# A mixture of experts in quarter blocks: four experts share one block, and the norm tiles of two projections are re-staged

## The chip, the cores and the metric

The kernel runs on one core of one Trainium2 chip. A core has TensorE (PE, matmuls into PSUM), VectorE (DVE), ScalarE (ACT), GpSimd (POOL) and SyncE (SP, which only issues DMAs here), and 16 DMA engines. The metric is the device time of one execution in microseconds; the median of three runs is shown. All data are fp32. An "fp32r" matmul is a faster one on rounded operands: three of them on high and low parts stand for one full fp32 product. A plain fp32 matmul with 512 moving columns appears in the trace as two records.

## The reference

Two blocks follow each other on 1024 tokens of 1024 channels. The part that changes most is the mixture of experts of the first block:

```python
scores = sigmoid(h @ router_w)                  # 64 experts
_, top_e = top_k(masked(scores + router_b), 8)  # 8 experts for each token
gate = gate / sum(gate) * 2.5
# tokens sorted by expert, in blocks of one expert each
def step(out, (tok, gw, e)):
    y = (silu(h[tok] @ wg[e]) * (h[tok] @ wu[e])) @ wd[e] * gw[:, None]
    return out.at[tok].add(y), None
return swiglu(h, shared) + routed
```

wg and wu are 1024 x 256 for each expert, wd 256 x 1024: 3.15 MB an expert, 201 MB for all. Before it come the first block's projection (rmsnorm, then `@ w_in`), two recurrences (rwkv and hgrn) and the output projection; behind it `x + g2 * moe`, a norm, and the second block, which begins with another rmsnorm and `@ w_in_2`.

## The kernel before

The program is a row of stages, each with its own instruction order written out by hand for every engine, tied by semaphores. Between stages all engines meet. The stages that matter here:

- `project_first` (names `front_`). It has two halves of 640 tokens. For each half, five tiles of 128 rows (one of them smaller) are normed by ScalarE and VectorE (`norm`), turned by TensorE into PSUM (`turn`, L530), and split into `a_high` and `a_low`. Then `product(s)` goes over the column tiles of the weight, two column halves c of 24 fp32r matmuls each (L548), into the banks `ps`; further banks, `aux`, serve the small lora products in between. The turned rows are put into `ps` too, so a half's turning waits until all products of the half before are taken out.
- `output_route` (names `out_`). It is the output projection, the second norm, the router, and the table that lists for each expert the tokens that chose it. An expert has room for 1024 tokens, rows of 128 places. SP loads the rows of tile i+3 while tile i is computed.
- `shared_expert`. It has the shared expert's matmuls in plain fp32 (L2324). It stores its result into `total` in DRAM; meanwhile VectorE turns the counts into the table of blocks: `owner[j]`, the expert of block j, `slots[:, j]`, its 128 tokens, and `done[e]`, the first block of expert e. Places that no token fills point at a row behind the last.
- `routed_experts` (names `routed_`, and `moe_exp_w` for the ring with the weights of four experts). It always runs 127 blocks, the number that the worst routing could need. Each block has 128 slots of one expert. Blocks behind the last used one belong to expert 63 and do unused work. In block j, TensorE turns the 128 gathered rows of block j+1 (L2526, 8 transposes), multiplies block j's x by the up and gate weights (L2559: 8 depth tiles by three fp32r products, x stationary with 128 columns, 512 weight columns moving, into `p_gu`), then block j−1's hidden rows by the down weights (L2541 and L2542), and turns block j's hidden rows (L2568). ScalarE rounds the weights to `w_high` (L2585, four pieces) and `wd_high`, VectorE subtracts to `w_low` (L2649) and `wd_low`. GpSimd gathers rows three blocks ahead (L2494, indirect DMA) and adds each result into `total` by an indirect DMA that accumulates (L2503). SP refills a ring entry when `done` says that its expert's last block has been used, the up and gate weights first, then the down weights.
- the second block's projection (names `pre_`). For each of eight tiles VectorE multiplies `total` with a gain and adds `x` (L3655, L3667), norms it twice, and TensorE turns it (L3523); then come the products (L3510). Products of two weight tiles are placed between the last turns. GpSimd splits these weights.

## Time and profile before

| | |
|---|---|
| median of 3 runs | 4236.89 us (4229.92 to 4244.08) |
| profiled execution, its own time | 4234.69 us |
| its span | 4232.8 us, mean granted clock 0.935 |
| PE / DVE / ACT / POOL busy | 86% / 63% / 48% / 21% |
| moved by DMA | 690.96 MB, 163 GB/s |
| loop over the experts | from 1794 to 3094 us |

The span is from the first to the last instruction. Busy time is a union per engine; a matmul's end is modelled, and overlapping ones make the "mean ns" of one longer than the distance of two starts. The slices of the page are 105.8 us each. PEclk is the granted TensorE clock, 1.00 being 2.4 GHz and 0.50 1.2 GHz.

### The profile page before, as it was taken

How to read it: one execution, taken by the hardware profiler on the slowest of the kernel's cores; microseconds unless marked ns; L12 is line 12 of the kernel's file. 1: busy time of each engine (PE TensorE's matmuls, PEld its weight loads, DVE VectorE, ACT ScalarE, POOL GpSimd, SP SyncE). 2: the span in 40 equal slices, each digit the busy share in tenths (PEclk: the TensorE clock that was granted, in tenths of full speed). 3: DMA queues.
4: the chain of work that ended last, by engine and by line, in shares of the span. 5: the costliest groups of instructions: out<-in, count | busy, mean ns of one | idle time of the engine just before them, and what ended most of it. 6: DMA issues, size and time to landing. Idle time of an engine off the chain costs nothing. (4 is left out here: it accounts for less than half of the span.)

```text
span 4232.8 us, 93615 instructions
## 1 busy us (share of the span) xinstructions
PE 3643.4 (86%) x35448; PEld 2938.0 (69%) x35449; DVE 2676.3 (63%) x4120; ACT 2044.4 (48%) x2837; POOL 907.3 (21%) x799
## 2 busy tenths in 40 slices
PE   4899799678776679799999999999949989968779
PEld 0898788577676557377777677777737767856667
DVE  2588688555555566287777777777768666036731
ACT  1477576322222153077777777777742222136720
POOL 3000000134433003323223233322213333300000
PEclk6899899799899789899999999999969999989989
DMA  8254344322210635499999999754563421355552
GB/s 302 76 172 155 116 159 153 128 68 56 81 54 9 216 136 138 154 318 270 277 342 341 341 338 340 190 108 108 111 168 90 119 75 60 110 139 134 131 169 80
DMA packets 527112, 690.96 MB, mean 163 GB/s; under 512 B 77904, under 2 KB 424656, under 8 KB 523728
## 3 DMA queue, kind: packets, MB, share of 16 engines
q1 hardware_dynamic: 487232, 545.70, 40.5%
q0 software_dynamic: 39088, 139.12, 13.4%
q8 instruction: 240, 3.93, 0.4%
q10 hardware_dynamic: 480, 1.62, 0.1%
q14 instruction: 72, 0.59, 0.0%
HBM read 508.35 MB, written 178.00 MB: 162 GB/s over the span
## 5 line engine op out<-in xcount | busy, mean ns | idle before, releaser
L2649 DVE TENSOR_TENSOR routed_w_low<-moe_exp_w,routed_w_high 128x1024 fp32r<-128x1024 f32 x512 | 603.0, 1219 | 26.8 <-ACT routed_w_high L2585 23.5
L2585 ACT CAST routed_w_high<-moe_exp_w 128x1024 fp32r x512 | 510.9, 1045 | 61.7 <-DMA moe_exp_w<-in_exp_w_up_dram 26.0
L2503 POOL DMA_INDIRECT total<-routed_y,routed_yidx x127 | 238.0, 1874 | 825.6 <-ACT routed_y L2610 304.4
L2559 PE MATMUL routed_p_gu<-routed_w_high,routed_x_high 128*128 128x512 f32 x1016 | 415.0, 408 | 0.0
L2559 PE MATMUL routed_p_gu<-routed_w_low,routed_x_high 128*128 128x512 f32 x1016 | 404.1, 398 | 0.0
L2559 PE MATMUL routed_p_gu<-routed_w_high,routed_x_low 128*128 128x512 f32 x1016 | 404.0, 398 | 0.0
L548 PE MATMUL front_ps<-front_a_high,front_w_high 128*128 128x320 f32 (+1 forms) x1120 | 363.5, 325 | 16.7 <-DVE front_w_low L785 13.5
L548 PE MATMUL front_ps<-front_a_high,front_w_low 128*128 128x320 f32 (+1 forms) x1120 | 355.2, 317 | 0.0
L548 PE MATMUL front_ps<-front_a_low,front_w_high 128*128 128x320 f32 (+1 forms) x1120 | 355.0, 317 | 0.0
L3510 PE MATMUL pre_ps<-pre_a_high,pre_w_high 128*128 128x512 f32 x720 | 287.7, 400 | 15.3 <-ACT pre_xb L3644 6.6
L3510 PE MATMUL pre_ps<-pre_a_low,pre_w_high 128*128 128x512 f32 x720 | 281.7, 391 | 0.0
L3510 PE MATMUL pre_ps<-pre_a_high,pre_w_low 128*128 128x512 f32 x720 | 281.7, 391 | 0.0
L2542 PE MATMUL routed_p_y<-routed_wd,routed_hT_rest 128*128 x508 | 260.2, 593 | 0.0
L1427 POOL TENSOR_TENSOR rwmix_TT<-rwmix_at,rw_mask 64x256 f32<-64x256 f32 (+1 forms) x60 | 43.4, 724 | 944.4 <-DVE rwmix_at L1328 938.5
L548 PEld LDWEIGHTS front_ps<-front_a_high,front_w_high 128*128 128x128 f32 x1120 | 214.3, 191 | 35.5 <-DVE front_w_low L785 18.1
L2559 PEld LDWEIGHTS routed_p_gu<-routed_w_high,routed_x_low 128*128 128x128 f32 x1016 | 192.1, 189 | 46.7
L2559 PEld LDWEIGHTS routed_p_gu<-routed_w_low,routed_x_high 128*128 128x128 f32 x1016 | 192.9, 190 | 41.0
L2559 PEld LDWEIGHTS routed_p_gu<-routed_w_high,routed_x_high 128*128 128x128 f32 x1016 | 192.9, 190 | 41.1
L548 PEld LDWEIGHTS front_ps<-front_a_low,front_w_high 128*128 128x128 f32 x1120 | 214.2, 191 | 1.3
L548 PEld LDWEIGHTS front_ps<-front_a_high,front_w_low 128*128 128x128 f32 x1120 | 213.9, 191 | 0.0
L2494 POOL DMA_INDIRECT moe_xg<-yn,moe_idx x128 | 157.8, 1233 | 104.5 <-DVE moe_idx L2638 53.7
L3510 PEld LDWEIGHTS pre_ps<-pre_a_high,pre_w_high 128*128 128x128 f32 x720 | 136.2, 189 | 48.7 <-issue 18.1
(556 smaller groups left out, 8362.3 us busy)
## 6 DMA issues: line engine op xcount, KB each, us to landing
moe_exp_w<-in_exp_w_gate_dram SPq DMA_DIRECT2D x64, 1024.0 KB, 14.4
moe_exp_w<-in_exp_w_up_dram SPq DMA_DIRECT2D x64, 1024.0 KB, 19.3
routed_wd<-in_exp_w_down_dram SPq DMA_DIRECT2D x64, 1024.0 KB, 15.5
front_wt<-in_w_in_dram SPq DMA_DIRECT2D x70, 512.0 KB, 4.3
mod_w<-in_w_mod_dram SPq DMA_DIRECT2D x24, 1024.0 KB, 18.1
pre_wt<-in_w_in_dram SPq DMA_DIRECT2D x44, 512.0 KB, 4.1
out_a<-mix SPq DMA_DIRECT2D x24, 512.0 KB, 4.4
proj<-pre_xv SPq DMA_DIRECT2D x16, 512.0 KB, 2.6
```

Source lines behind the costliest of these rows:

```text
L548: op = nc.tensor.matmul(ps[:, s % 2, c, 0:size], w_part[:, s % 2, k, :], a_part[:, k, first + c * size:first + (c + 1) * size], start=(k = ...
L1427: nc.gpsimd.tensor_tensor(combos(TT[u][:])[to, es], combos(at[u][:])[at_rows, es], mask(MASK_LEVEL, at_rows, es), ALU.mult)
L2494: nc.gpsimd.indirect_dma_start(xg[:, b % 2, :], None, yn, bass.IndirectOffsetOnAxis(ap=idx[b][:, :], axis=0))\
L2503: nc.gpsimd.indirect_dma_start(total, bass.IndirectOffsetOnAxis(ap=yidx[b % 2][:, :], axis=0), y[:, b % 2, :], None, compute_op=ALU.add).t ...
L2542: op = nc.tensor.matmul(p_y[:, h, :], hT_rest[:, :], wd[:, bass.ds(e % WS, 1), 1, cols], start=False, stop=True)
L2559: op = nc.tensor.matmul(p_gu[:, :], x_part, w_part[:, k, :], start=(k == 0 and i == 0), stop=(k == KD - 1 and i == 2))
L2585: nc.scalar.copy(w_high[:, q * KQ:(q + 1) * KQ, :].rearrange("p k m -> p (k m)"), wgu[:, bass.ds(e % WS, 1), q * KQ:(q + 1) * KQ].rearrang ...
L2649: nc.vector.tensor_tensor(w_low[:, at, :].rearrange("p k m -> p (k m)"), wgu[:, bass.ds(e % WS, 1), at].rearrange("p o k j m -> p (o k j m)"),
L3510: op = nc.tensor.matmul(ps[:, u, a:a + n], w_part[:, u, k, :], a_part[:, k, a:a + n], start=(k == 0 and j == 0), stop=(k == KD - 1 and j = ...
```

## The change

**The loop over the experts.** Blocks of 128 slots become "quads": four quarters of 32 slots, each of its own expert (consecutive quarters in the sorted list, so often the same expert). Their number is 80, again the worst case. A matmul's stationary operand is now x of one quarter, 32 columns, and its result goes to 32 partitions of the PSUM bank: four matmuls in a row, for the spots 0 to 3, have the same depth and different columns of the array. All are plain fp32; the splits into high and low parts are gone. Only spot 0 reads its weights from the ring at an address in a register; those of the other three spots are copied to a fixed ring `fixed` of four steps, spot 1 by ScalarE, spots 2 and 3 by VectorE. A quad has six steps: four pairs of depth tiles on the way up, two on the way down; `chunk_done` counts them and frees the places. SP refills an entry after the quad that holds the expert's last quarter; up weights of expert e+3, then down weights of expert e.

**The sums.** The same token could stand in two quarters of one quad, so each spot adds into its own part of `total`. Parts 1 to 3 are cleared in `output_route` by three DMAs from a tile of zeros (1024 x 1024 fp32 each). The second block's norm loads all four parts of a tile and adds them on TensorE with the identity as stationary operand (`sums_of`), and VectorE takes the sum from PSUM.

**The table.** Its rows have 32 places; four indirect DMAs in place of one fetch them, and owners are turned four times.

**The first projection.** The turned rows go into the `aux` banks instead of `ps`. So `ps` is free under the norm, and the first column half of the first two weight tiles is computed before the last two turned tiles of each half. VectorE's `bonus` of the last column tile of the first half is moved ahead of the second norm, since it reads `aux`.

TensorE in the routed loop, one block of the kernel before, from the turns on (a block is an expert's 128 slots; w_high, w_low and x_high, x_low are the parts; the three products then come seven times more):

```order
L2568 MATMUL routed_p_h<-ident,routed_hid 128x128 x2
L2526 MATMUL routed_p_x<-ident,moe_xg 128x128 x8
L2559 MATMUL routed_p_gu<-routed_w_high,routed_x_high 128x512
L2559 MATMUL routed_p_gu<-routed_w_low,routed_x_high 128x512
L2559 MATMUL routed_p_gu<-routed_w_high,routed_x_low 128x512
```

and one quad of the kernel after, where moe_exp_w is spot 0's weight in the ring and routed_fixed those of spots 1 to 3 (this pair then comes seven times more):

```order
L2638 MATMUL routed_p_h<-ident,routed_hid 128x128 x2
L2589 MATMUL routed_p_x<-ident,moe_xg 128x128 x8
L2492 TENSOR_LOAD moe_owner
L2492 ISA x2
L2608 ISA
L2608 MATMUL routed_p_gu<-moe_exp_w,routed_x 32x512
L2608 MATMUL routed_p_gu<-routed_fixed,routed_x 32x512 x3
```

Three products of 128 columns give way to four of 32 for each depth tile.

VectorE in the same loop, from the turned rows' gates on; before (routed_w_low is the low part of a quarter of the up weights, routed_wd_low that of the down weights):

```order
L2642 COPY routed_gate<-moe_xg 128x1
L2643 TENSOR_TENSOR routed_x_low<-routed_p_x,routed_x_high 128x1024
L2638 CAST moe_idx<-moe_slots 128x1
L2458 TENSOR_LOAD moe_owner
L2458 ISA x2
L2656 ISA
L2656 TENSOR_TENSOR routed_wd_low<-routed_wd,routed_wd_high 128x1024
L2649 ISA
L2649 TENSOR_TENSOR routed_w_low<-moe_exp_w,routed_w_high 128x1024
```

and after, around the multiplication that makes the hidden rows:

```order
L2742 ISA
L2742 COPY routed_fixed<-routed_wd 128x1024
L2726 ISA x4
L2730 ISA
L2730 COPY routed_fixed<-moe_exp_w 128x1024
...
L2771 TENSOR_TENSOR routed_hid<-routed_sg,routed_p_gu 128x256
L2748 CAST routed_yidx<-moe_slots 128x1
```

Each step has two copies where it had one subtraction, and an address in a register before each; behind the last row six more such copies follow.

TensorE in the second block's norm; before, five turned tiles stand together ahead of the first product:

```order
L3523 MATMUL pre_aux<-ident,pre_yb 128x128 x40
L3510 MATMUL pre_ps<-pre_a_high,pre_w_high 128x512
```

and after, with the sums of the four parts (pre_buf and pre_wide hold the parts of even and odd tiles):

```order
L3619 MATMUL pre_ps<-pre_buf,ident 128x512 x8
L3619 MATMUL pre_ps<-pre_wide,ident 128x512 x8
L3635 MATMUL pre_aux<-ident,pre_yb 128x128 x8
L3619 MATMUL pre_ps<-pre_buf,ident 128x512 x8
L3635 MATMUL pre_aux<-ident,pre_yb 128x128 x8
L3619 MATMUL pre_ps<-pre_wide,ident 128x512 x8
```

The sum of tile t+1 stands behind the turn of tile t−1 and ahead of the turn of tile t.

The diff, cut to its core:

```diff
@@ project_first, tensor
             def turn(half):
                 if half:
-                    pe.wait_ge(evicted, PER)
+                    pe.wait_ge(aux_act, 5 * QT)
+                    pe.wait_ge(aux_dve, 2 * QT)
                 for j, (src, idx) in enumerate(sources[half]):
                     t, size = half * NT + j, src.shape[0]
+                    if j >= NT - 2:
+                        early(half * PER + j - (NT - 2))
                     pe.wait_ge(y_made, t + 1)
...
+            def early(s):
+                pe.wait_ge(w_split, s + 1)
+                if s >= PER:
+                    pe.wait_ge(evicted, s - 1)
+                pe.wait_ge(low_made, s // PER * NT + 3)
+                columns(s, 0)
@@ output_route, sync
+                if 1 <= i < SPOTS:
+                    sp.dma_start(total[i * PART:i * PART + SEQ, :].rearrange("(p r) (a l) -> p (r a) l", p=P, l=P),
+                                 none[:].rearrange("p (o l) -> p o l", o=1).broadcast_to([P, SEQ * D // P // P, P])).then_inc(none_sent, 16)
@@ sizes
-BLOCKS = SEQ * TOP_K // P + N_EXPERTS
-USED = (SEQ * TOP_K + (P - 1) * N_EXPERTS + N_EXPERTS - TOP_K) // P
+SPOTS = 4
+QUARTER = P // SPOTS
+QUADS = (SEQ * TOP_K + (QUARTER - 1) * N_EXPERTS + N_EXPERTS - TOP_K) // QUARTER // SPOTS + 1
+PART = SEQ + QUARTER
@@ routed_experts, sync
+            def next_first(e, at, w):
+                quad = sp.value_load(tb["done"][0:1, at], min_val=0, max_val=NB - 2)
+                sp.wait_ge(chunk_done, quad * STEP + CH)
+                first(e, w)
+            def next_second(e, at, w):
+                quad = sp.value_load(tb["done"][0:1, at], min_val=0, max_val=NB - 2)
+                sp.wait_ge(chunk_done, quad * STEP + 2 * STEP)
+                second(e, w)
...
+                    next_first(i * WS + (w + WS - 1), only(i * WS + w), (w + WS - 1) % WS)
+                    next_second(i * WS + w, only(i * WS + (w - WS + 1)), w)
@@ routed_experts, tensor
+            def up(j, b):
+                e = owner(pe, j, 0)
+                pe.wait_ge(x_made, j + 1)
...
+                for c in range(CH):
+                    copies(up_step(j, c))
+                    for k in range(c * KC, (c + 1) * KC):
+                        cols = slice((k - c * KC) * BANK, (k - c * KC + 1) * BANK)
+                        for s in range(SPOTS):
+                            w = wgu[:, bass.ds(e % WS, 1), k * BANK:(k + 1) * BANK] if s == 0 else fixed[:, place_of(b, c), s - 1, cols]
+                            op = nc.tensor.matmul(p_gu[spot(s), :], x[:, b % 2, k, spot(s)], w, start=(k == 0), stop=(k == KD - 1))
...
+                for m in range(MT):
+                    copies(down_step(j, m))
...
+                            op = nc.tensor.matmul(p_y[spot(s), h, :], hT[:, m, spot(s)], w, start=(m == 0), stop=(m == MT - 1))
@@ routed_experts, vector
+            def up_copies(es, j, b, c):
+                g = up_step(j, c)
...
+                    dve.wait_ge(chunk_done, g - (R - 1))
+                for s in (2, 3):
+                    op = nc.vector.tensor_copy(fixed[:, place_of(b, c), s - 1, :],
+                                               wgu[:, bass.ds(es[s] % WS, 1), c * D:(c + 1) * D].rearrange("p o n -> p (o n)"))
@@ second block's projection, tensor
+            def sums_of(t):
+                pe.wait_ge(parts_ready[t % 2], 16 * SPOTS * (t // 2 + 1))
+                if t >= 1:
+                    pe.wait_ge(part_made, t)
+                for a in range(2):
+                    for j in range(SPOTS):
+                        op = nc.tensor.matmul(ps[:, a, BANK:2 * BANK], consts["ident"][:, :], parts_t[t % 2][j][:, a * BANK:(a + 1) * BANK],
+                                              start=(j == 0), stop=(j == SPOTS - 1))
+                op.then_inc(summed, 1)
@@ second block's projection, vector
             def gained(t):
-                dve.wait_ge(x_ready[t % 4], 32 * (t // 4 + 1))
-                nc.vector.tensor_tensor(total_t[t % 4][:, :], total_t[t % 4][:, :], gain_row[:, :], ALU.mult).then_inc(part_made, 1)
+                dve.wait_ge(summed, t + 1)
+                for a in range(2):
+                    cols = slice(a * BANK, (a + 1) * BANK)
+                    op = nc.vector.tensor_tensor(spread[:, t % 2, cols], ps[:, a, BANK:2 * BANK], gain_row[:, cols], ALU.mult)
```

## Rows read from the trace of the kernel before

**Rows 1.** The page: TensorE's busy tenths and GB/s in 40 slices.
```profile
PE   4899799678776679799999999999949989968779
GB/s 302 76 172 155 116 159 153 128 68 56 81 54 9 216 136 138 154 318 270 277 342 341 341 338 340 190 108 108 111 168 90 119 75 60 110 139 134 131 169 80
```

**Rows 2.** Windows of the loop: busy us (count) by engine, granted clock, DMA share, GB/s.
```profile
core 0: us, PE busy (x) PEld busy (x) DVE busy (x) ACT busy (x) POOL busy (x), PEclk, DMA share, GB/s
2094.00:2194.00 100.00, 93.81 (x413) 70.23 (x412) 71.48 (x102) 69.06 (x93) 27.59 (x18) 0.98 1.07 338
...
2860.00:3060.00 200.00, 200.00 (x897) 151.91 (x896) 156.13 (x224) 154.47 (x205) 56.88 (x41) 1.00 0.50 108
```

**Rows 3.** Timeline of TensorE over one block: start, length, instruction.
```profile
2809.70 1.04 PE L2526 MATMUL routed_p_x<-ident,moe_xg 128*128 128x128 f32 x8
2810.49 0.48 PE L2559 MATMUL routed_p_gu<-routed_w_high,routed_x_high 128*128 128x512 f32 x1
...
2816.20 0.39 PE L2541 MATMUL routed_p_y<-routed_wd_high,routed_hT_high 128*128 128x512 f32 x1
...
2819.30 0.38 PE L2568 MATMUL routed_p_h<-ident,routed_hid 128*128 128x128 f32 x2
2819.52 0.71 PE L2526 MATMUL routed_p_x<-ident,moe_xg 128*128 128x128 f32 x5
```

**Rows 4.** The page's costliest groups: count, busy us, mean ns, idle before.
```profile
L2649 DVE TENSOR_TENSOR routed_w_low<-moe_exp_w,routed_w_high 128x1024 fp32r<-128x1024 f32 x512 | 603.0, 1219 | 26.8 <-ACT routed_w_high L2585 23.5
L2585 ACT CAST routed_w_high<-moe_exp_w 128x1024 fp32r x512 | 510.9, 1045 | 61.7 <-DMA moe_exp_w<-in_exp_w_up_dram 26.0
L2503 POOL DMA_INDIRECT total<-routed_y,routed_yidx x127 | 238.0, 1874 | 825.6 <-ACT routed_y L2610 304.4
...
L2494 POOL DMA_INDIRECT moe_xg<-yn,moe_idx x128 | 157.8, 1233 | 104.5 <-DVE moe_idx L2638 53.7
```

**Rows 5.** Timeline of TensorE at four places: rows of equal matmuls.
```profile
999.91 0.67 PE L1144 MATMUL rwmix_ps<-rwmix_TT,rwmix_W 64*64 64x64 f32 x30
...
1767.78 19.05 PE L2324 MATMUL shared_pd<-shared_wd,shared_hid 128*128 128x512 f32 x44
...
3804.94 1.31 PE L2893 MATMUL attn_po<-attn_pT,attn_v 128*64 128x128 f32 x20
...
3951.83 1.39 PE L3172 MATMUL ssd_pb<-ssd_sq,ones 128*128 128x128 f32 x11
```

**Rows 6.** Groups of TensorE by form, for the mean length of one.
```profile
L1144 PE MATMUL rwmix_ps<-rwmix_TT,rwmix_W 64*64 64x64 f32 x3200 | 73.0, 225 | 14.8 <-DVE rwmix_W L1344 9.7 <-issue 5.0
...
L2893 PE MATMUL attn_po<-attn_pT,attn_v 128*64 128x128 f32 x576 | 38.5, 278 | 0.8 <-DVE attn_res L2944 0.5
...
L2324 PE MATMUL shared_pd<-shared_wd,shared_hid 128*128 128x512 f32 x64 | 27.7, 592 | 0.0
...
L3172 PE MATMUL ssd_pb<-ssd_sq,ones 128*128 128x128 f32 x128 | 17.3, 293 | 2.4 <-ACT ssd_sq L3228 2.4
```

**Rows 7.** One tile of the second projection: ns min/median/max, first and last start.
```profile
L3724 DVE TENSOR_SCALAR pre_buf<-pre_aux x8: 1217/1224/1225, 3228.8 to 3332.2; 128x1024 f32<-128x1024 f32 x8
...
L3734 DVE TENSOR_SCALAR pre_buf<-pre_buf x4: 693/694/695, 3376.4 to 3574.4; 128x1024 f32<-128x1024 f32 x4
```

**Rows 8.** Timeline of VectorE and GpSimd in the second norm.
```profile
3127.33 3.13 POOL L3502 TENSOR_TENSOR pre_w_low<-pre_wt,pre_w_high 128x1024 fp32r<-128x1024 f32 x1 [0.15 <-issue]
...
3128.30 3.25 DVE L3671 TENSOR_TENSOR pre_xv<-pre_xb,pre_xc 128x1024 f32<-128x1024 f32 x1
```

**Rows 9.** DMA issues of the loop: count, KB each, median us to landing.
```profile
routed_wd<-in_exp_w_down_dram SPq DMA_DIRECT2D x64, 1024.0 KB, 15.5
```

**Rows 10.** Timeline of TensorE in the second norm, with its wait.
```profile
3144.19 1.97 PE L3523 MATMUL pre_aux<-ident,pre_yb 128*128 128x128 f32 x8 [4.68 <-DVE pre_yb L3685]
3150.84 1.97 PE L3523 MATMUL pre_aux<-ident,pre_yb 128*128 128x128 f32 x8 [4.69 <-DVE pre_yb L3685]
```

**Rows 11.** Windows of 10 us in the three norms (columns as in rows 2).
```profile
120.00:130.00 10.00, 8.44 (x43) 8.28 (x43) 1.31 (x3) 1.87 (x2) 0.00 (x0) 0.64 0.28 77
...
450.00:460.00 10.00, 5.13 (x24) 4.58 (x25) 6.93 (x10) 4.76 (x7) 0.00 (x0) 0.50 0.21 72
...
3140.00:3150.00 10.00, 1.97 (x8) 1.57 (x8) 9.40 (x14) 7.30 (x12) 0.00 (x0) 0.50 0.74 202
```

More of the change, by code:

```diff
@@ L2248, in shared_expert @@
         cnt_i = st.sb("cnt_i", [P, 2, NE], I32)
-        nb, cmp, end, start, one = (st.sb(n, [P, NE]) for n in ("nb", "cmp", "end", "start", "one"))
-        lane = st.sb("lane", [P, 1])
-        own = st.sb("own", [P, 5])
-        row = st.sb("row", [P, 1], U32)
+        nb, end, start, one = (st.sb(n, [P, NE]) for n in ("nb", "end", "start", "one"))
+        cmp = st.sb("cmp", [P, SPOTS, NE])
+        lane, behind = st.sb("lane", [P, SPOTS]), st.sb("behind", [P, 1])
+        own = st.sb("own", [P, 5, SPOTS])
+        row = st.sb("row", [P, SPOTS], U32)
         places = st.sb("places", [P, P])
@@ L2317, in _ @@
             pe.wait_ge(own_made, 1)
-            nc.tensor.transpose(own_row, own[:, 0:1], consts["ident"][:, :]).then_inc(turned, 1)
+            for j in range(SPOTS):
+                op = nc.tensor.transpose(own_row[:, j * P:(j + 1) * P], own[:, 0, j:j + 1], consts["ident"][:, :])
+            op.then_inc(turned, 1)
             for c in range(DOWN):
@@ L2347, in _ @@
             nc.vector.memset(one[:, :], 1.0)
-            nc.vector.memset(tb["slots"][:, BLOCKS:, :], 0.0)
-            nc.vector.memset(tb["owner"][0:1, BLOCKS:], NE - 1)
+            for j in range(SPOTS):
+                nc.vector.memset(behind[j * QUARTER:(j + 1) * QUARTER, :], float(j * PART))
             for c in range(BEGUN):
@@ new lines, in down @@
+            def down(j, b):
+                e = owner(pe, j, 0)
+                pe.wait_ge(hT_made, j + 1)
+                if not begins(j):
+                    pe.wait_ge(y_made, j)
+                for m in range(MT):
+                    copies(down_step(j, m))
+                    at = place_of(0, m) if ends(j) else place_of(b + 1, CH + m)
+                    for h in range(2):
+                        cols = slice(h * BANK, (h + 1) * BANK)
+                        for s in range(SPOTS):
+                            w = wd[:, bass.ds(e % WS, 1), m, cols] if s == 0 else fixed[:, at, s - 1, cols]
+                            op = nc.tensor.matmul(p_y[spot(s), h, :], hT[:, m, spot(s)], w, start=(m == 0), stop=(m == MT - 1))
+                    op.then_inc(chunk_done, 1)
@@ L2562, in body @@
-                if not first:
-                    down(j - 1)
+                if not ends(j):
+                    turn(j + 1, (b + 1) % BS, r + (b + 1) // BS)
+                up(j, b)
+                if not begins(j):
+                    down(j - 1, (b - 1) % BS)
                 pe.wait_ge(hid_made, j + 1)
-                if not first:
-                    pe.wait_ge(h_split, j)
+                if not begins(j):
+                    pe.wait_ge(hT_made, j)
                 for k in range(MT):
@@ new lines, in down_copies @@
+            def down_copies(j, b):
+                e, last = owner(act, j, 1), owner(act, j, SPOTS - 1)
+                for w in range(WS):
+                    act.wait_ge(second_loaded[w], (last + (WS - w)) // WS * 16 + (16 if w else 0))
+                for m in range(MT):
+                    act.wait_ge(chunk_done, down_step(j, m) - (R - 1))
+                    at = place_of(0, m) if ends(j) else place_of(b + 1, CH + m)
+                    nc.scalar.copy(fixed[:, at, 0, :], wd[:, bass.ds(e % WS, 1), m, :].rearrange("p o n -> p (o n)"))\
+                        .then_inc(first_copied, 1)
@@ L2664, in _ @@
             indices(2, 2)
[L2665 to L2668 removed]
+            es = [owner(dve, 0, s) for s in range(SPOTS)]
+            gates(es, 0, 0)
+            for c in range(CH):
+                up_copies(es, 0, 0, c)
             def body(j, b, r):
[L2671 removed]
+                es = [owner(dve, j + 1, s) for s in range(SPOTS)]
                 if not isinstance(j, int) or j >= BS - 1:
```

396 lines of the change are left out of this document (210 added, 186 removed).

## The prediction

> **What bounds the kernel now.** I read the busy slices of the page first [rows 1]: the longest stage with a constant picture is slices 17 to 29, where TensorE is at 9 of 10 throughout. That is the loop over the chosen experts. The windows cut it up [rows 2]: it runs from 1794 to 3094 us, 1300 us, 31% of the span. Its second half (2860 to 3060) has TensorE busy for all of 200 us at 108 GB/s. From 2094 it has 338 GB/s and more and TensorE is short of full by 6%. So TensorE bounds the loop, and while weights still arrive the DMA nearly does.
>
> The timeline of one block [rows 3] gives the price of a block: from one set of turns (2809.70) to the next (2819.52) 9.82 us. The multiplications start 0.234 us apart, from 2810.49 to 2816.20 for 24 of them. The loop runs 127 blocks [rows 4]: 127 × 9.82 = 1247, and 53 us are start and stalls. VectorE and ScalarE are at 78 and 77% there.
>
> The profiled execution's own time is 4234.7 us (span 4232.8), 2 us under the median of 4236.9. I count against 4234.7.
>
> **The loop: TensorE per quad.** A quad is 128 slots of up to four experts. The turns of x and of the hidden rows stay: 2810.49 − 2809.70 = 0.79, and 0.22 for the two others [rows 3]. In place of 24 fp32r multiplications and 8 for the way down come 32 and 16 in plain fp32, each 32 columns wide with 512 moving. What would one cost alone? 44 recorded halves of such multiplications take 19.05 us, the last of them 0.59 [rows 5, 6]: (19.05 − 0.59)/43 = 0.429 us a half, 0.858 for the whole. The question on which everything hangs is how many of the four run side by side. Recorded halves on a whole array with 128 moving columns stand (1.39 − 0.29)/10 = 0.110 us apart; those of attention, on two column halves at full depth, (1.31 − 0.27)/19 = 0.055: two abreast, nothing lost. The rwkv ones, on 64 × 64 tiles, stand (0.67 − 0.22)/29 = 0.0155 apart with 64 moving columns, where one alone would need 0.055: 3.5 abreast [rows 5, 6]. No row shows four column tiles at full depth. Bounds: 12 steps × 0.858 = 10.3 us if four run together, 20.6 if two do. I take 10.3, since nothing is lost with two at full depth and four have run at once, and 11.8 (10.3 × 4/3.5) as the poor end. A quad is then 10.3 + 0.79 + 0.22, with 0.1 for changes of tile form, 11.4 us; 80 quads (the new count) are 912 us instead of 1247.
>
> The Trainium skill (TensorE: Matmul & The Clock Gate, "Part 3: Packing small matmuls") measures 2.38 times for three column tiles, and 10.6 for sixteen. By 2.38/3 a quad would be 10.3/0.79 + 1.1 = 14.1 us and the total, worked out as below, 4192; this trace has two tiles without such a loss, and does not show four.
>
> **The loop: copies.** The splits into high and low parts go; three of the four experts' weights are copied into a fixed ring, 6 chunks of 128x1024 a quad. ScalarE copies one expert: 6 × 1.045 [rows 4]. Its block of now is 9.82 × 0.77 = 7.6 us [rows 2] with five such casts, so one more makes 8.7. VectorE copies two: 12 copies. The nearest rows, one input in SBUF and 128x1024, take 0.694; the same from PSUM 1.22 [rows 7]. I take 0.69, since the copies are from SBUF: 8.3, and seven small operations, 1.3 in all: 9.6 us. Both lie under TensorE's 11.4. VectorE's bad end is 12 × 1.22 + 1.3 = 15.9. Before a copy's address is known the engine loads the owner into a register, six loads instead of two on VectorE; I leave 1 us for them, still under 11.4.
>
> **The loop: DMA.** A block gathers and scatters 1.08 MB (108 GB/s in the windows × 9.82), a quad the same. An expert's weights are 3.15 MB. At the ceiling of 340 GB/s [rows 2] and 13 us a quad, 83 GB/s go to rows and 257 to weights: 12.2 us an expert. The first half of the loop now runs at that ceiling. The reference's own routing gives these inputs 26 to 455 tokens an expert: 288 quarters, so 72 of the 80 quads hold tokens. 24 experts have 5 or more quarters (40.25 quads, TensorE sets 11.4 × 40.25 = 459), 40 have four or fewer (the DMA sets 40 × 12.2 = 488), 8 empty quads 91: 1038. The ring looks three experts ahead, which evens some of it out; against that, a down weight is now queued behind the next 2 MB, and lands in 15.5 us already now [rows 9], where it has one quad. I add 20 for it and 12 for the start: 1070. The term: 1070 − 1300 = −230 us. Its bounds: −375 if only TensorE counts (912 + 12), −110 if each small expert costs another 3 us.
>
> **The second block's norm.** The four partial sums are added on TensorE, 16 halves of 0.429 a tile: 6.9 us at 2.4 GHz, 13.7 at 1.2. The cycle of a tile is 3150.84 − 3144.19 = 6.65 us now [rows 10], with TensorE waiting. In the order after, the sum of tile t+1 stands behind the turn of t−1, VectorE takes it before it finishes tile t, and the next turn waits for that: 0.8 + 6.9 + 1.4 (two of 128x512 from PSUM, half of 1.22 each and a little) + 1.5 + 0.4 = 11.0. Seven cycles × 4.35 = 30. The two products that fill waits now (24 × 0.234 = 5.6 each) are no longer hidden: 11. The first two sums run where the granted clock is 0.50 [rows 11]: 19. Sum +60; +45 if they are partly hidden, +100 if the clock stays at 1.2 GHz.
>
> **Zeros.** Three further parts are cleared, 12.6 MB, 37 us at 340 GB/s, from the same queue as the rows of the output projection. That stage moves 138 GB/s [rows 1] and loads three tiles ahead. +5, from 0 to +37. What is fetched in four pieces behind the table costs +3.
>
> **The first projection.** Under each of the two norms the first columns of two weight tiles move into TensorE's waits. Now it stands idle or turns rows at a granted 0.50 until about 121 and 460 us [rows 11]. Moved are 2 × 24 multiplications at 320/512 of 0.234, 7 us at each norm, 14 in all; the last turned rows are now queued behind them, and VectorE's norm behind those, which I put at 1 us each: −12, from −20 to +2 (if the norm chain is delayed by as much as was moved).
>
> Sum: 4234.7 − 230 + 60 + 5 + 3 − 12 = 4060.7; the median of runs stood 2 us above: **4062 us**.
>
> **Rivals.**
> - *Two abreast.* The four matmuls of a step share the array only in pairs: 21.7 us a quad, 80 × 21.7 + 12 = 1748, total 4235 + 448 + 56 = 4739. For it: no row has more than two column tiles on one set of rows. Against it: four rwkv tiles at once. It makes the kernel slower from 15.4 us a quad on (1244 for the loop). 9%.
> - *VectorE and GpSimd on each other.* While GpSimd ran a 3.13 us operation, a VectorE one of 1.22 took 3.25 [rows 8]. GpSimd's two indirect DMAs take 1.23 + 1.87 us a quad [rows 4]. If VectorE's copies drop to 1.22, it is 80 × 15.9 + 12 = 1284, total 4275, slower; it decides from 1.17 a copy. If the two only take turns, VectorE's 10.6 and GpSimd's 3.1, it is 13.7 a quad, 1108 for the loop, 4101 in all. Against both: the subtractions take 1.219 on average with GpSimd's DMAs beside them [rows 4]. Copies at 1.22: 6%; turns: 4%.
>  The Trainium skill (SBUF — State Buffer, "SBUF: two separate sides") says that an fp32 copy on VectorE locks GpSimd out of a shared port, and measures an indirect-style DMA at 3100 instead of 620 ns. Five times 3.1 would be 15.5 us a quad and 4243 in all. The trace has no such copy beside an indirect DMA.
> - *A short pack.* Four tiles reach 3.5, as the rwkv ones did: 12.9 us a quad, 40.25 × 12.9 + 488 + 8 × 12.9 + 32 = 1142, total 4135. For it: those same rows. Against it: their matmuls are an eighth as long, so a fixed cost weighs more. 10%.
> - *The DMA is no bound.* The ring evens out large and small experts: 924, total 3915. For it: averaged, 190 + 78 MB at 340 GB/s are 788 us, less than TensorE's 821 for 72 quads. 8%.
> - *DMA queues bind more than I count*: 1190, total 4181. For it: weights now land after 15.5 us. 11%.
> - My forecast: 52%.
>
> **Chances and range.** Of the 85 that lie on the fast side (forecast 52, queues 11, short pack 10, no DMA bound 8, turns 4) I leave 3 for several bad bounds meeting, so that nothing measurable is left: faster 82%, no change 3% (0.3%, 13 us, is what a measurement tells here). Slower 15%: two abreast 9, VectorE at 1.22 6. The range takes the forecast with the bounds of its terms and all cases but the slower ones: 3910 to 4210.
>
> **What would show it.** The multiplications of the loop in groups of four within about 20 ns, the groups 0.43 us apart; or pairs. Quads 11.4 us apart from the 72nd on, and 12 to 14 before, with DMA at 340 GB/s and TensorE waiting for copies whose releaser is a weight's DMA. VectorE's copy at 0.69. In the norm, tiles 11 us apart with sums in between. The first columns before the last turned rows. It would be wrong if quads without tokens stood more than 12.8 apart, or if VectorE were never idle in the loop.

## The result and the profile after

| | before | after |
|---|---|---|
| median of 6 runs each | 4233.41 us (4228.34 to 4257.26) | 4261.5 us (4256.74 to 4263.24) |
| ratio to before, 95% interval | | 1.0055 (1.0034 to 1.0076) |
| span / own time of the profiled execution | 4232.8 / 4234.7 | 4254.7 / 4257.0 |

The changed kernel is slower by 0.55%. I had forecast 4062 us. From where each stage starts and ends on the two timelines, the stages take:

| stage, us | before | after | difference | forecast |
|---|---|---|---|---|
| first projection and rwkv, to the end of rwkv | 1379.5 | 1357.4 | −22 | −12 |
| output projection and routing, to the shared expert | 177.7 | 206.7 | +29 | +5 |
| shared expert | 62.1 | 63.4 | +1 | +3 |
| loop over the chosen experts | 1301 | 1248 | −53 | −230 |
| second projection | 614.3 | 674.8 | +60.5 | +60 |
| all else (attention, ssd) | | | +6 | 0 |

The page of the kernel after: TensorE is no longer at 9 throughout in the loop (slices 17 to 28), the granted clock is below full there, and in slices 21 to 25 the DMA, at 338 to 342 GB/s before [rows 1], now moves 243 to 319.

```profile
PE   4998999587775877788868877889779999968779
...
PEclk6999999899897888899988988899889999989889
...
GB/s 302 93 156 173 113 178 128 129 68 54 77 41 76 158 210 169 158 266 195 169 319 249 243 283 275 223 215 116 130 181 86 119 76 64 105 140 141 120 168 79
...
q14 instruction: 162, 1.33, 0.1%
```

The question on which I said everything hangs was answered as forecast. Timeline of TensorE in the loop after: start, length, instruction (the second row stands for three). A group of four starts within 20 ns, the next 0.43 us later.

```profile
2799.50 0.59 PE L2608 MATMUL routed_p_gu<-moe_exp_w,routed_x 128*32 x1
2799.51 0.61 PE L2608 MATMUL routed_p_gu<-routed_fixed,routed_x 128*32 128x512 f32 x3
2799.93 0.59 PE L2608 MATMUL routed_p_gu<-moe_exp_w,routed_x 128*32 x1
```

The groups that answer to [rows 4]: the copies are as short as I took them (685 and 689 ns), GpSimd's scatter is shorter than before, and what is new is how long TensorE and VectorE stand ahead of what concerns `routed_wd`, the down weights.

```profile
L2623 PE MATMUL routed_p_y<-routed_wd,routed_hT 128*32 x640 | 353.5, 705 | 233.8 <-DVE routed_fixed L2742 226.0
...
L2730 DVE COPY routed_fixed<-moe_exp_w 128x1024 f32 x640 | 403.5, 685 | 32.0 <-PE routed_p_y L2623 25.4
...
L2742 DVE COPY routed_fixed<-routed_wd 128x1024 f32 x320 | 200.2, 689 | 299.1 <-DMA routed_wd<-in_exp_w_down_dram 182.0
...
L2565 POOL DMA_INDIRECT total<-routed_y,routed_yidx x80 | 126.5, 1581 | 901.4 <-ACT routed_y L2679 867.1
```

The waits from 1900 to 3000 by what ended them (us in total, times, longest) show that ScalarE stands there too:

```profile
ACT routed_fixed L2673 <- DMA routed_wd<-in_exp_w_down_dram: 234.2, 24, 19.1
PE routed_p_y L2623 <- DVE routed_fixed L2742: 206.2, 30, 15.9
DVE routed_fixed L2742 <- DMA routed_wd<-in_exp_w_down_dram: 163.6, 24, 18.1
```

One of those waits on the timeline of all engines. SyncE asks for gate and up weights of an expert three ahead at 1866 and only then, at 1870.45, for down weights; they are there at 1887. TensorE, done with its up step at 1873, waits 16 us and then takes 0.85 us a group instead of 0.43.

```profile
1866.63 2.57 SPq L2514 DMA_DIRECT2D moe_exp_w<-in_exp_w_up_dram  x1
...
1870.45 7.45 SPq L2518 DMA_DIRECT2D routed_wd<-in_exp_w_down_dram  x1
...
1887.60 2.50 DVE L2742 COPY routed_fixed<-routed_wd 128x1024 f32 x4 [18.38 <-DMA routed_wd<-in_exp_w_down_dram]
...
1889.29 1.06 PE L2623 MATMUL routed_p_y<-routed_wd,routed_hT 128*32 x1 [15.97 <-DVE routed_fixed L2742]
...
1890.14 1.06 PE L2623 MATMUL routed_p_y<-routed_wd,routed_hT 128*32 x1
```

The windows there (us, busy by engine, granted clock, DMA share, GB/s) show the clock at 1.00 before the wait and at 0.50 behind it, that is 1.2 instead of 2.4 GHz; this wait cost more than its length.

```profile
1866.00:1873.00 7.00, 7.00 (x67) 2.06 (x65) 2.29 (x8) 2.47 (x4) 2.55 (x2) 1.00 1.07 371
1889.00:1892.00 3.00, 2.71 (x16) 0.76 (x20) 3.00 (x7) 2.53 (x4) 0.00 (x0) 0.50 1.08 371
```

### The profile page after: what moved, and what is told of

Read it like the earlier page. It is cut to its first block and busy times, and to the rows that moved or that the text cites. A ratio compares the mean times of both kernels' runs of the same rounds, so it can differ in the third digit from the quotient of the medians.

```text
span 4254.7 us, 100492 instructions
## 1 busy us (share of the span) xinstructions
PE 3463.0 (81%) x38463; PEld 2353.4 (55%) x38464; DVE 2362.8 (56%) x4246; ACT 1763.5 (41%) x2362; POOL 716.3 (17%) x706
## 3 DMA queue, kind: packets, MB, share of 16 engines
q14 instruction: 162, 1.33, 0.1%
## 5 line engine op out<-in xcount | busy, mean ns | idle before, releaser
L2608 PE MATMUL routed_p_gu<-routed_fixed,routed_x 128*32 128x512 f32 x3840 | 567.3, 595 | 0.0
L2608 PE MATMUL routed_p_gu<-moe_exp_w,routed_x 128*32 x1280 | 566.2, 595 | 0.7 <-DVE routed_fixed L2730 0.7
L2623 PE MATMUL routed_p_y<-routed_wd,routed_hT 128*32 x640 | 353.5, 705 | 233.8 <-DVE routed_fixed L2742 226.0
L2662 ACT COPY routed_fixed<-moe_exp_w 128x1024 f32 x320 | 334.0, 1046 | 261.2 <-PE routed_p_y L2623 162.0
L2730 DVE COPY routed_fixed<-moe_exp_w 128x1024 f32 x640 | 403.5, 685 | 32.0 <-PE routed_p_y L2623 25.4
L2742 DVE COPY routed_fixed<-routed_wd 128x1024 f32 x320 | 200.2, 689 | 299.1 <-DMA routed_wd<-in_exp_w_down_dram 182.0
L2623 PE MATMUL routed_p_y<-routed_fixed,routed_hT 128*32 128x512 f32 x1920 | 354.4, 704 | 0.0
L2608 PEld LDWEIGHTS routed_p_gu<-moe_exp_w,routed_x 128*32 128x32 f32 x1280 | 134.5, 110 | 351.0 <-issue 351.0
L2673 ACT COPY routed_fixed<-routed_wd 128x1024 f32 x160 | 164.8, 1045 | 287.5 <-DMA routed_wd<-in_exp_w_down_dram 253.2
L2565 POOL DMA_INDIRECT total<-routed_y,routed_yidx x80 | 126.5, 1581 | 901.4 <-ACT routed_y L2679 867.1
```

The costliest lines, as they stand in the source:

```text
L2565: nc.gpsimd.indirect_dma_start(total, bass.IndirectOffsetOnAxis(ap=yidx[b % 2][:, :], axis=0), y[:, b % 2, :], None, compute_op=ALU.add).t ...
L2608: op = nc.tensor.matmul(p_gu[spot(s), :], x[:, b % 2, k, spot(s)], w, start=(k == 0), stop=(k == KD - 1))
L2623: op = nc.tensor.matmul(p_y[spot(s), h, :], hT[:, m, spot(s)], w, start=(m == 0), stop=(m == MT - 1))
L2662: nc.scalar.copy(fixed[:, place_of(b, c), 0, :], wgu[:, bass.ds(e % WS, 1), c * D:(c + 1) * D].rearrange("p o n -> p (o n)"))\
L2673: nc.scalar.copy(fixed[:, at, 0, :], wd[:, bass.ds(e % WS, 1), m, :].rearrange("p o n -> p (o n)"))\
L2730: op = nc.vector.tensor_copy(fixed[:, place_of(b, c), s - 1, :], wgu[:, bass.ds(es[s] % WS, 1), c * D:(c + 1) * D].rearrange("p o n -> p ( ...
```

## The experiments

Ratios are to the kernel before on the same chip, with their 95% interval. The times of stages come from each kernel's one profile.

### The loop: what a quad costs, and the down weights

**e2_no_weights.** Edit: `first(e, w)` and `second(e, w)` in the loop become `sp.sem_inc(loaded[w], 32)` and `sp.sem_inc(second_loaded[w], 16)`.

> Leaves out the loading of the routed experts' weights but for the first four experts (the first four's are used for all); copies, multiplications, gathers and scatters stay. It measures what the quads cost without weight traffic. By my sum 80 quads at 11.4 us and 12 us of start: 924 us. If four column tiles side by side or the copies cost more than I worked out, it is 1000 us or more; if copies or the scatters set the pace, the quads stand 12 us or more apart.

Measured: 4058.95 us in one run, loop 1053 us. Neither account fits alone: the distance from one quad's turns to the next is 11.68 us, near my 11.4, but every fourth is 17.1 to 18.7. The timeline of VectorE over three of the quads: ahead of its first work in a new round of the loop it stands 4.80 us, where the others have 1.33 and 0.95; ahead of the copies for the way down (L2742) it stands 1.9 to 2.6 us each time.

```profile
2413.06 0.62 DVE L2719 COPY routed_gate<-moe_xg 32x1 f32 x4 [1.33 <-issue]
...
2415.76 2.50 DVE L2742 COPY routed_fixed<-routed_wd 128x1024 f32 x4 [1.89 <-issue]
...
2424.42 0.62 DVE L2719 COPY routed_gate<-moe_xg 32x1 f32 x4 [0.95 <-ACT routed_y L2679]
...
2427.22 2.50 DVE L2742 COPY routed_fixed<-routed_wd 128x1024 f32 x4 [2.00 <-issue]
...
2439.72 0.62 DVE L2719 COPY routed_gate<-moe_xg 32x1 f32 x4 [4.80 <-issue]
...
2443.13 2.50 DVE L2742 COPY routed_fixed<-routed_wd 128x1024 f32 x4 [2.60 <-issue]
```

The DMA view of 2431 to 2440 has three pieces of instructions (packets, MB, share), which start at 2431.6, 2434.1 and 2436.6, just ahead of the restart at 2439.72; from 2400 to 2600 there are 19, five for each round of the loop, and in the same stretch of the kernel before the queue has no row at all.

```profile
q14 instruction: 3, 0.02, 1.0%
```

TensorE then waits for the copies, and its granted clock is 0.50 from 2443.4 to 2450.3:

```profile
2444.73 1.05 PE L2623 MATMUL routed_p_y<-routed_wd,routed_hT 128*32 x1 [3.77 <-DVE routed_fixed L2742]
...
2445.57 1.06 PE L2623 MATMUL routed_p_y<-routed_wd,routed_hT 128*32 x1
```

**e1_down_first.**

```diff
-                    next_first(i * WS + (w + WS - 1), ...)
                     next_second(i * WS + w, ...)
+                    next_first(i * WS + (w + WS - 1), ...)
```

> The changed kernel, with the down weights of an expert asked for ahead of the gate and up weights of the expert three further on (SyncE's two requests in the loop change places; same bytes, same instructions elsewhere). Theory, the order in the queue: the changed kernel asks for expert e's down weights only after e-1's last up chunk and behind 2 MB, where they are needed one quad later, though their slot had been free for long; TensorE then waits some 230 us for them. With the request earlier these waits go, and the loop falls from 1248 us to about 1050 (960 to 1080, my old sum without the 20 us for the queue), the total to about 4060. Rival, the bandwidth: the bytes can't come faster than they do, so the waits move to the gate and up weights, the loop stays above 1200 and the total above 4210.

Measured: 4137.69 us, ratio 0.9767 (0.9750 to 0.9784); loop 1135 us, 113 less than in the changed kernel. Shown: the order of two requests cost 113 us, and the bandwidth rival falls. VectorE's waits for down weights from 1900 to 2800, in the changed kernel and here:

```profile
DVE routed_fixed L2742 <- DMA routed_wd<-in_exp_w_down_dram: 153.5, 22, 18.1
...
DVE routed_fixed L2742 <- DMA routed_wd<-in_exp_w_down_dram: 60.9, 18, 10.3
```

I had expected 198 us and a loop of 1080 at most: a miss. The fourth quads that e2 showed are still there, at 17.2 to 25 us.

**e7_short_body** (on e1) **and e10_short_body_alone** (on the changed kernel). VectorE's loop body of four quads becomes one of two; index and gate columns are then addressed by a register:

```diff
-            turns(dve, body)
+            with dve.Fori(BS // PAIR, NB // PAIR - BS // PAIR) as i:
+                for b in range(PAIR):
+                    body(i * PAIR + b, b, i)
...
-                nc.vector.tensor_copy(idx[b][:, :], ...)
+                nc.vector.tensor_copy(idx_all[:, bass.ds(j % BS, 1)], ...)
```

> Down weights asked for first, and VectorE's loop over the quads written with a body of two quads instead of four (158 instructions of its list instead of 304; 36 returns to the loop's start instead of 18; the same operations in the same order, index and gate columns addressed by a register). Theory, the instructions: in the run without weight traffic each quad stands 11.68 us from the next but every fourth, where VectorE's loop starts over, stands 17.1 to 18.7; 8 KB pieces of instructions come in there, VectorE stands for 4.8 us, TensorE waits for its copies and goes on at half clock. The kernel before (134 instructions) has no such place. With a body that needs no fetching every quad is 11.68 apart, the loop falls from 1135 to about 1000 (960 to 1035: 80 x 11.68 + 12 = 946, and what the weights cost), the total to 4000 (3970 to 4040). Rival, the return itself: each return of a loop with registers to set costs VectorE some 4 us; twice as many returns then make the loop about 100 us longer, 1235. Second rival, VectorE is too full and loses its lead slowly: no change.

> The changed kernel with VectorE's shorter body alone, down weights still asked for last. If the two causes add, the loop falls from 1248 us by what the body costs, 17 or 18 times 6 to 9 us: about 1120 (1090 to 1150), total about 4135. If the waits for the down weights hide the fetching (VectorE waits there anyway), it falls by less than 60 us.

Measured: e7 4066.15 us, ratio 0.9606 (0.9582 to 0.9629), loop 1056; e10 4187.62 us, ratio 0.9894 (0.9869 to 0.9918), loop 1174. Both loops are longer than the ranges I gave. The two causes add: the short body is worth 79 us with the down weights asked for first and 74 without, the order 118 with the short body and 113 without. The pieces of instructions are gone from the loop (76 over the whole span instead of 162), and the rival of 4 us for each return falls. The quads are not yet 11.68 but mostly 12.0 and 12.6 to 13.4 in turn.

**e12_one_wait** (on e7) and **e14_one_wait_long_body** (on e1, body of four kept). VectorE's eight waits a quad for weights become two:

```diff
+                act.sem_inc(up_here, 1)          # ScalarE, behind its own waits
...
-                    for w in range(WS):
-                        dve.wait_ge(loaded[w], (es[-1] + (WS - w)) // WS * 32 + (16 if w else 0))
+                    dve.wait_ge(up_here, j + 1)  # the same for second_loaded / down_here
```

> As e7 (down weights first, body of two quads), but VectorE waits for an expert's weights through one semaphore that ScalarE raises after its own eight waits, instead of eight waits of its own with a threshold worked out in registers: 142 instructions instead of 158 (ScalarE's 198 become 206). Theory: in e7 a pair of quads takes 12.0 and 12.6 to 13.4 us where nothing is fetched, because VectorE stands up to 3.2 us in register work ahead of its copies for the way down, and TensorE waits 1.5; with less of it the quads fall to 11.68 where the DMA is not at its ceiling, and the loop by 15 to 30 us. Rival: the DMA sets the loop (338 GB/s from 2130 to 2630): within 8 us.

> As e12 but with VectorE's body of four quads: down weights first, one wait instead of eight, 272 instructions in the body (304 in the changed kernel, 261 in the long body of the kernel before that fetched nothing, 142 in e12). If the fetching begins between 261 and 272 the 8 KB pieces and the 17 us quads are back and the loop is 1090 to 1110; if it begins between 272 and 304 the loop is as in e12, 1030, or some us less, since no column is addressed by a register.

Measured: e12 4040.36 us, ratio 0.9531 (0.9511 to 0.9550), loop 1030. e14 4027.65 us, ratio 0.9503 (0.9484 to 0.9523), loop 1026, no piece of instructions between 1910 and 2775, and 59 of its 78 distances are 11.68. A body of four quads is therefore not fetched again as such: with 272 instructions it is not, with 304 it is. That length alone decides is not shown, since a changed body also begins and ends at other places of VectorE's program, and no run moved one without changing its length. Of the 81 us by which e14's distances exceed 11.68, 70 lie in seven quads of 18.5 to 23 us; ScalarE still waits for the DMA of up and down weights there, up to 13.7 us. Windows of e14: TensorE busy 97.5 to 100 of 100 at full clock, with the DMA at 332 to 334 GB/s in the middle.

```profile
2000.00:2100.00 100.00, 97.54 (x888) 33.79 (x880) 68.51 (x153) 67.70 (x80) 22.60 (x18) 1.00 0.84 247
2240.00:2340.00 100.00, 97.60 (x888) 33.45 (x880) 69.81 (x159) 69.99 (x82) 23.59 (x18) 1.00 1.05 334
2480.00:2580.00 100.00, 99.80 (x906) 34.96 (x902) 74.13 (x164) 72.87 (x87) 20.95 (x16) 1.00 1.05 332
2700.00:2800.00 100.00, 100.00 (x916) 34.60 (x908) 74.59 (x162) 73.01 (x85) 20.37 (x16) 1.00 0.42 87
```

**e11_before_long_body.** In the kernel before, VectorE's loop gets a body of eight blocks (`for b in range(2 * BS): body(i * 2 * BS + b, b % BS, i * 2 + b // BS)`).

> The kernel before, with VectorE's loop over the blocks written with a body of eight blocks instead of four: 261 instructions of its list instead of 134, 14 returns to the start instead of 30, everything else the same. Theory, the instructions: a body this long has to be fetched again at each return (in the changed kernel 304 had to, 158 not), so 8 KB pieces appear in the loop, and VectorE stands some 5 us at each of 14 returns; the blocks there last 14 to 16 us instead of 9.82, the loop about 14 x 5 = 70 us longer (30 to 100), the total 4290 (+1.4%). If 261 still fit, nothing changes (within 0.2%). Rival, the return itself costs: fewer returns, so the same or less.

Measured: 4233.85 us, ratio 0.9992 (0.9976 to 1.0007). I had expected a loss: a miss. No instructions are fetched from 2000 to 3000: 261 instructions in the body, as e14's 272, stay.

### The second block's norm

**e5_one_part** and **e9_one_product** (both on the changed kernel). `for j in range(SPOTS)` becomes `range(1)`, in the loads and the products, or in the products alone; both leave out three of the four parts.

> The changed kernel with three of the four partial sums left out of the second block's norm: neither loaded nor added (one identity product per half tile stays). If the stage is longer by its 16 halves a tile and their loads, it falls from 675 us to 620 to 630, and the cycle of a tile from 15.8 to 7 to 8 us.

> The changed kernel with all four parts loaded in the second block's norm but only one of them added: 12 of 16 halves on TensorE left out. My forecast put the whole of the stage's growth on TensorE: then it falls as far as with one part loaded. Rival, the loads: the trace shows TensorE waiting 38 us for the parts, which have two buffers only, so the cycle stays above 12 us and the stage above 650.

Measured, each in one run: e5 4211.67 us, stage 633.4 (−41), cycle of a tile 10.9; e9 4254.39 us, stage 665.4 (−9), cycle 15.7. A cycle is here the mean of the six distances between the first seven turned tiles, 15.8 us in the changed kernel and 8.1 in the one before. The sums on TensorE, which I held for all of it, are 9 us of the 41, and 7 of the 9 lie ahead of the first turned tile; the stages of the other kernels with the same norm lie between 670 and 683, so the 9 is rough. Even with one part the stage is 19 us longer than before; no run takes that apart. SyncE's timeline in the changed kernel shows why the loads weigh: tile 3's parts (`pre_wide`) are asked for at 3102.22, though tile 1's sum, which frees their buffer, was over at 3092; ahead of them stands the wait for the store of `h`.

```profile
3091.31 1.93 SPq L3529 DMA_DIRECT2D pre_buf<-total  x4
3094.53 0.32 SPq L3572 DMA_DIRECT2D h<-pre_xb  x1
...
3102.22 1.86 SPq L3529 DMA_DIRECT2D pre_wide<-total  x4
3112.64 0.32 SPq L3572 DMA_DIRECT2D h<-pre_xb  x1
...
3121.26 2.01 SPq L3529 DMA_DIRECT2D pre_buf<-total  x4
```

**e13_norm_order** (on e12).

```diff
+            sp.wait_ge(summed, 1)
+            sums_of(2)
             params(0)
             for t in range(LAT_TILES):
-                if t + 2 < LAT_TILES:
-                    sp.wait_ge(summed, t + 1)
-                    sums_of(t + 2)
+                if t + 3 < LAT_TILES:
+                    sp.wait_ge(summed, t + 2)
+                    sums_of(t + 3)
                 sp.wait_ge(h_made, t + 1)
```

> As e12, and in the second block's norm SyncE asks for the parts of tile t+3 as soon as tile t+1 is added, ahead of the parameter columns and of its wait for the store of tile t. Theory, the order of the requests: three of four sums on TensorE left out gave 9 us, three of four parts left out 41, and SyncE asks for a tile's parts some 10 us after their buffer is free, because they stand behind a wait and 5 to 7 us of small requests. With the request at once the cycle of a tile falls from 15.8 to 12 or 13 us, the stage from 675 to about 650 (640 to 658), the total to 4017. Rival, the bytes: 2.6 MB a tile at what the queue moves; then the stage stays within 6 us.

Measured: 4023.71 us, ratio 0.9508 (0.9492 to 0.9524), against e12's 4040.36; the intervals of the two ratios overlap. Stage 661.6 (−13; 661.8 in e15, which has the same order), cycle 13.7. The place of the request is part of the cause, about half of what I expected of it; the rest of the 32 us that the loads cost stays open between bytes and two buffers.

### Clearing the parts, and the first projection

**e3_zeros_early**, **e6_first_and_early** (with e1's edit), **e8_body_zeros_late** (on e7), **e15_and_zeros_early** (on e13). The three clearing DMAs move into the rwkv stage (e3, e6, e15), or from `if 1 <= i < SPOTS` to `if i > NT - SPOTS`, behind the last tiles (e8).

> The changed kernel, with the three parts cleared during the rwkv stage, where the DMA moves 54 to 86 GB/s, not during the output projection. Theory: the clearing, 12.6 MB from the queue that brings the projection's rows, is what made that stage 207 us instead of 178; it falls by 25 to 29 us, the rwkv stage stays within 3 us, total -22 to -29 (0.5 to 0.7%). Rival: the stage is longer for its other edits (GpSimd's table of 32-slot blocks) and the time stays, or the rwkv stage loses what this one gains: within 0.2%.

> Both edits: down weights asked for first, parts cleared in the rwkv stage. If the two are independent the gains add: about 4035 us (3950 to 4060), faster than both kernels by 4 to 6%. If the bandwidth rival holds for the first, about 4200.

> As the last, and the three parts cleared behind token tiles 5, 6 and 7 of the output projection's stage instead of 1, 2 and 3: there the DMA stands at 8 to 67% and no rows of the projection are queued behind. Theory, the queue: the stage takes 207 us because 12.6 MB stand ahead of the projection's rows in SyncE's queue; moved behind them it takes 178 to 185, the total 20 to 29 us less than the last run. Rival, the bytes: wherever they stand they cost about the same, as in the rwkv stage (31 gained, 17 lost); or the gate rows of the routing queue behind them: within 10 us of the last run.

> As e13, with the three parts cleared in the rwkv stage as in e3, where that gave 31 us in the output projection and took 17 in the rwkv stage. If the bytes cost in both places what they did there, the total is 10 to 15 us under e13; if the gain of e3 was chance, the same as e13.

Measured:

| | time, us | ratio to before | output stage | rwkv stage |
|---|---|---|---|---|
| after | 4261.5 | 1.0055 (1.0034 to 1.0076) | 206.7 | 586 |
| e3 | 4250.41 | 1.0044 (1.0028 to 1.0061) | 175.5 | 603 |
| e1 / e6 | 4137.69 / 4135.47 | 0.9767 / 0.9764 (0.9748 to 0.9781) | 203.6 / 175.9 | 591 / 609 |
| e7 / e8 | 4066.15 / 4065.35 | 0.9606 / 0.9606 (0.9588 to 0.9624) | 200.0 / 199.3 | 592 / 598 |
| e13 / e15 | 4023.71 / 4005.39 | 0.9508 / 0.9468 (0.9449 to 0.9488) | 202.6 / 175.2 | 584 / 600 |

The clearing costs the output stage 27 to 31 us: shown. My account that the queue's order is to blame falls: moved behind the projection's rows it costs the same (e8). In its windows the DMA is full for the last 80 us of the stage, and in the last 40 TensorE is nearly out of work. The DMA engines are full there at 143 and 184 GB/s, not at 340.

```profile
1660.00:1700.00 40.00, 34.68 (x139) 22.26 (x138) 24.46 (x130) 6.59 (x10) 21.85 (x23) 0.91 1.17 143
1700.00:1740.00 40.00, 6.66 (x16) 2.75 (x16) 0.94 (x7) 0.27 (x1) 7.55 (x9) 0.62 0.97 184
```

In the rwkv stage the clearing costs 16 to 18 us by the pairs; without it that stage takes 583 to 598 us in the other runs of the changed kernel and its variants, with it 600 to 609. Over the whole kernel moving it there gained, by the ratios, 5, 1 and 17 us in three pairs; only the last pair has intervals apart. Both expectations missed: e3 was to gain 22 to 29 us, with nothing lost in the rwkv stage, and e6 was to take 4035 us, a sum that also held too large a gain from e1's edit. How it slows the rwkv stage, whose DMA is at 27% of its time, stays open.

**e4_front_only.** The kernel before with the new `project_first` alone.

> The kernel before with the change of the first projection alone (turned rows in the other banks, the first columns of two weight tiles under each norm). My forecast was 12 us less, -20 to +2. The trace of the changed kernel has that stage 18 us shorter and the rwkv stage behind it 4 us shorter. If it is worth what the stage shows, the total is 4215 (-18, 0.4%); if the rwkv stage gives part of it back, within 0.2%.

Measured: 4223.02 us, ratio 0.9979 (0.9965 to 0.9992): −9 us (−15 to −3), near my −12. The profiles have the first projection 17 to 18 us shorter, more than the whole kernel gained; where the rest goes stays open. Windows of the kernel after, for [rows 11]: the clock rises between 110 and 120 us, where the kernel before has 0.50, and 0.64 still from 120 to 130.

```profile
100.00:110.00 10.00, 5.08 (x22) 4.68 (x23) 8.03 (x12) 4.79 (x9) 0.00 (x0) 0.50 0.70 102
110.00:120.00 10.00, 8.85 (x60) 8.44 (x59) 7.30 (x9) 3.29 (x6) 0.00 (x0) 0.91 0.75 122
120.00:130.00 10.00, 9.14 (x52) 9.14 (x53) 1.98 (x3) 3.22 (x5) 0.00 (x0) 0.83 0.07 16
```

e15 is the best version run: 5.3% (5.1 to 5.5) faster than the kernel before.

## Why the prediction was wrong

- **The step that failed: "a down weight is now queued behind the next 2 MB ... I add 20 for it".** The mechanism was named and mis-sized: 113 to 118 us (e1, e7 against e10). I took it as a delay that happens once. VectorE waited for down weights 24 times between 1900 and 3000, and TensorE restarted at 1.2 GHz behind the wait shown. My own rival "DMA queues bind more", 1190 for the loop, had this mechanism, though not its size. The rival of slow copies came nearer in total (4275), for a reason that did not occur: they took 0.685 us, not 1.22.
- **The step that was missing: the length of VectorE's loop.** 134 instructions became 304; fetching them again in its 18 rounds cost 74 to 79 us with the waits it caused. No row of the kernel before could price it, but the code showed the growth. Together with the 1056 us that e7 takes, the two make up the loop: 1056 + 118 + 74 = 1248. The sign I had named for being wrong, quads without tokens more than 12.8 us apart, came: one of the last eight took 16.8, the others 11.68. The Trainium skill has the rule (Runtime: NRT & Kernel Launch, "Instruction fetch mechanics"): a taken branch whose target lies outside a window of two pages has to wait for a DMA. The trace agrees with the mechanism, not with the sizes: pieces here are 8 KB (1.33 MB in 162), and a body of 304 instructions is fetched again where the page's 32 KiB would hold 512.
- **TensorE per quad: right.** Four abreast without loss, 11.68 us a quad against my 11.4 (0.28 × 80 = 22 us short). Two abreast and the short pack are excluded. So is the Trainium skill's ratio for three tiles (TensorE: Matmul & The Clock Gate, "Part 3: Packing small matmuls"): groups 0.43 us apart are what one alone takes.
- **Copies: right in length, wrong in what surrounds them.** 0.685 us. Both rivals on the shared port are out as I priced them, since quads stand 11.68 us apart. But "I leave 1 us for them, still under 11.4" was wrong: about two to three us of register work stand right ahead of the copies for the way down, where TensorE waits next. I compared sums of busy time, and the place in the quad decided. Two waits for eight were worth 26 us of the loop (e7 to e12).
- **VectorE and GpSimd on each other: hardly put to the test.** In the changed kernel only 2 of the 80 scatters met a copy; in the kernel before, the scatters that ran beside a subtraction for 0.8 us or more took 2.10 us on average, those with less than 0.3 us of it 1.58, which is what all take now (mean 1581 against 1874 ns). Where the two do meet, each is a little longer: in e14 copies that overlap a GpSimd DMA by 0.3 us or more take 0.76 us and those that meet none 0.68, and gathers beside copies for 0.8 us or more take 1.09 us instead of 0.98. That is far from the five times that I weighed from the Trainium skill (SBUF — State Buffer, "SBUF: two separate sides").
- **DMA: the sum came near, by two errors that offset.** 1070 less the 20 for the queue is 1050, and with both stalls gone the loop took 1056 (e7) and 1026 (e14). But I had made the 1050 of 912 for TensorE, 12 for the start and 126 for the DMA; in e14 80 quads at 11.68 are 934, and 92 are left for the start and all waits. Nearly all of it runs at TensorE's pace, at 332 to 334 GB/s in its middle; so the ring evened out more than I took. (108 GB/s over 9.82 us is 1.06 MB a block, not 1.08; it changes nothing here.)
- **Norm: the total right by luck, its working wrong.** +60.5 against +60. The 6.65 us that I read as the cycle now holds for three of seven distances; from the first to the last turned tile it is 50 us before and 98 after (+48, against my 30 and 11), and up to the first turned tile 19 and 33 (+14, against my 19, for which I showed no working). And the loads, not the sums, are most of it: of the 41 us that three parts cost, the sums are 9.
- **Zeros:** +29 where I took 5, inside my range. The 37 us that I called the upper end was worked out at 340 GB/s and is too low: in e3 a clearing DMA landed 17.6 us after its issue (the median of three), 53 for the three, and beside the projection's rows the stage's DMA share is 0.87 to 1.09.

With e1's and e14's edits alone the kernel is 5% faster than before, 206 us where I forecast 172 for the change; two stalls around it took more than that back.

## What to carry to other kernels

When a change makes blocks serve several owners, write down for every load when its buffer comes free and when it is asked for: twice here a request stood behind others in one queue's order long after its buffer was free (down weights 113 us, parts of the norm 13). Count the instructions of each engine's loop body before and after, and look for instruction packets in the DMA view: a body that was fetched again cost 4 to 5 us in each round here. An engine with a third of its time free can still be late where it matters, if its register work stands directly ahead of what the next engine waits for.

## What was not expected of the hardware

- VectorE's loop: bodies of 134, 142, 158, 261 and 272 instructions fetched nothing in the loop, 304 fetched five 8 KB pieces in each round, the first three about 2.5 us apart without weight traffic, with up to 4.8 us of standstill; with weights arriving beside it a fourth quad took mostly 20 to 22 us instead of 17 to 18.
- Four column tiles of 32 at full depth run plain fp32 halves with 512 moving columns side by side at 0.43 us.
- Around a wait of 3.8 us TensorE's granted clock was 0.50 for 6.8 us (groups 0.85 apart until 2449.84), and that quad took 6.7 us more than 11.68.
- 12.6 MB of zeros in 512-byte runs cost 27 to 31 us where the DMA was busy and 16 to 18 where it was at 20%; one of the three, 4.2 MB, took 17.6 us to land in the quieter stage.
- The DMA engines are full at 332 to 342 GB/s with weights, and at 143 to 184 GB/s while the zeros are written beside small rows (e8).
